# First expert rows by selection products, inverse roots on POOL

## The reference

```python
h = h + concat([pool_out, ssd_out]) @ w_out          # two mixers over rmsnorm(h) @ w_in
h = h + _hier_moe(_rmsnorm(h, norm_ffn), ...)        # top-1 of 4 groups, top-2 of its 8 experts
gate = sigmoid(_rmsnorm(h, norm_ple) @ ple_gate_w + ple_gate_b)
h = h + gate * (p @ ple_proj_w)
y = _rmsnorm(h, norm_final)
# _rmsnorm(x, g) = x * rsqrt(mean(x * x) + 1e-6) * g
```

## Time and profile before

| | |
|---|---|
| median of 3 runs | 585.47 us (584.82 to 586.27) |
| the profiled execution | 585.49 us |
| its span, first to last instruction | 583.6 us |
| mean granted TensorE clock | 0.958 |
| busy: TensorE, DVE, ACT, POOL | 510.3 (87%), 209.7 (36%), 170.7 (29%), 92.6 us (16%) |
| chain that ended last, share of the span | PE 72%, DMA 11%, DVE 8%, SP's queue 3%, ACT 3% |
| DMA moved | 144.72 MB, mean 248 GB/s |

### The profile page before, as it was taken

How to read it: one execution, slowest core, us unless ns; L and a number is a source line. 1 busy time by engine, 2 the same in 40 slices (tenths; PEclk the granted TensorE clock), 3 DMA queues, 4 the chain that set the end, 5 groups by cost and what they waited for, 6 DMA issues and landing times.

```text
span 583.6 us, 7814 instructions
## 1 busy us (share of the span) xinstructions
PE 510.3 (87%) x3098; PEld 314.5 (54%) x3098; DVE 209.7 (36%) x516; ACT 170.7 (29%) x345; POOL 92.6 (16%) x138
## 2 busy tenths in 40 slices
PE   2999978999999997099999999977849999799993
PEld 2888866768654655065555555533425553344452
DVE  2185694423022655441211221111111120565375
ACT  0635233203422423102222222221211223435255
POOL 1000053995000001101111112101111222000000
PEclk9999997999999999579999999999998999799998
DMA  8980000500629804949999999999999997700011
GB/s 322 417 238 2 1 1 0 217 2 19 212 95 419 352 2 182 414 151 356 417 419 416 414 414 418 414 416 418 416 404 388 414 411 293 295 2 0 1 74 72
DMA packets 39638, 144.72 MB, mean 248 GB/s; under 512 B 14458, under 2 KB 15098, under 8 KB 29988
## 3 DMA queue, kind: packets, MB, share of 16 engines
q1 hardware_dynamic: 32740, 132.79, 57.4%
q0 software_dynamic: 5152, 8.85, 4.1%
q10 hardware_dynamic: 1712, 2.62, 1.2%
HBM read 140.15 MB, written 14.19 MB: 264 GB/s over the span
## 4 chain that ended last, share of the span: by engine, by line
PE 72%; DMA 11%; DVE 8%; SPq 3%; ACT 3%; issue 2%; POOL 0%; POOLq 0%; DVEq 0%; ACTq 0%
PE PS L991 17%; PE PS L635 10%; PE PS L823 9%; PE PS L1012 9%; PE PS L1093 7%; PE PS L595 6%; PE PS L606 5%; DMA mem<-in_exp_w_down 5%; DVE mem L1871 2%; SPq L486 2%; PE PS L836 2%; DMA mem<-in_w_a 2%; DMA u_rows<-mem 2%; DVE mem L1615 1%; DMA mem<-u_rows,idx_all 1%
## 5 line engine op out<-in xcount | busy, mean ns | idle before, releaser
L991 PE MATMUL PS<-mem 128*64 128x256 f32 x512 | 118.8, 385 | 7.0 <-DVE mem L1871 7.0
L992 PE MATMUL PS<-mem 128*64 128x256 f32 x512 | 118.8, 385 | 0.0
L991 PEld LDWEIGHTS PS<-mem 128*64 128x64 f32 x512 | 68.2, 138 | 43.1 <-DVE mem L1871 7.9
L1012 PE MATMUL PS<-mem 128*64 128x512 f32 x256 | 62.6, 610 | 18.0 <-issue 8.9
L635 PE MATMUL PS<-mem 128*128 128x260 f32 x320 | 73.9, 387 | 0.0
L992 PEld LDWEIGHTS PS<-mem 128*64 128x64 f32 x512 | 68.2, 138 | 0.0
L635 PEld LDWEIGHTS PS<-mem 128*128 128x128 f32 x320 | 60.3, 192 | 10.7 <-issue 1.5
L595 PEld LDWEIGHTS PS<-mem 128*128 128x128 f32 (+4 forms) x254 | 33.3, 178 | 53.7 <-issue 36.3
L595 PE MATMUL PS<-mem 128*128 128x128 f32 (+4 forms) x254 | 42.6, 303 | 21.1 <-DMA mem<-u_rows,idx_all 12.6
L823 PE MATMUL PS<-mem 128*128 128x512 f32 x128 | 56.6, 595 | 0.0
L1875 DVE TENSOR_TENSOR mem<-PS,mem 64x256 f32<-64x256 f32 x32 | 13.7, 428 | 119.3 <-ACT mem L1291 119.3
(11 more groups left out here) (284 smaller groups left out, 541.4 us busy)
## 6 DMA issues: line engine op xcount, KB each, us to landing
mem<-in_exp_w_down SPq DMA_DIRECT2D x32, 1024.0 KB, 23.0
mem<-in_exp_w_gate SPq DMA_DIRECT2D x32, 1024.0 KB, 16.8
mem<-in_exp_w_up SPq DMA_DIRECT2D x32, 1024.0 KB, 20.2
mem<-in_w_out SPq DMA_DIRECT2D x2, 2048.0 KB, 7.6
mem<-in_ple_gate_w SPq DMA_DIRECT2D x1, 4096.0 KB, 30.3
mem<-choice_rows SPq DMA_DIRECT2D x4, 1024.0 KB, 8.3
mem<-in_xT SPq DMA_DIRECT2D x2, 1040.0 KB, 8.1
mem<-in_w_a SPq DMA_DIRECT2D x2, 1024.0 KB, 11.1
```

What stands on the lines that cost most here:

```text
L991: pe.matmul(PS[0][0:S, 0:FF], rows_k, gu[slot][:, k, :], start=(k == 0), stop=(k == KT - 1))
L992: ins = pe.matmul(PS[1][S:2 * S, 0:FF], rows_k, gu[slot][:, KT + k, :], start=(k == 0), stop=(k == KT - 1))
L1012: ins = pe.matmul(PS[4 + h][h * S:(h + 1) * S, :], actT[:, s % 2, f * S:(f + 1) * S], dn[slot][:, f, h * 512:(h + 1) * 512], start=(f == 0 ...
```

## The change

Three things. The rows of pair 0 no longer come from memory: for each token tile DVE writes a 0/1 matrix times the row's inverse root (`first_pair_rows`, which tells for each of 128 places which token sits there), and TensorE multiplies h1 by it (`first_pair`), which selects, scales and transposes at once, summed over the tiles in banks 0 and 2, which `first_pair_zero` clears. The slot table is summed in bank 3, not in 1. Gather 0 is left out, the second pair is transposed whole within block 1, and what concerns extra blocks moves behind block 0. And all inverse roots are an addition and a power of -0.5 on POOL; ACT's squares carry the 1/1024 in their scale. The order of the tail on ACT and DVE changes with it. The diff, cut (left out are semaphore names, the same wait in the loop by `gathers`, the body of `extra_choices`, which is L1829 to L1850 unchanged, and the tail's squares, which change as `half_square` does):

```diff
+def gathers(p):
+    return 16 * ((p + 1) // 2)
+
...
+C_POWER = C_EPS + 1
...
+        junk_h = at(R_g + D, D)
+        sel = at(R_g, NT, 2 * S)
+        selk = at(R_g + NT * 2 * S, 2, 2, S)
+        hit = at(R_g + (NT + 2) * 2 * S, 2, S)
...
+                        ins = pe.matmul(PS[3][q * S:(q + 1) * S, 0:MAIN], posh[:, j, :], choice[:, q, :],
...
+            SEL = [PS[0], PS[2]]
+
+            def first_pair_zero():
+
+                pe.wait_ge(s_outp_out, 9)
+                for half in range(2):
+                    pe.matmul(SEL[half][:, :], bef[:, 0:1].to_broadcast((P, P)), const[:, 0:256].bitcast(BF16),
+                              start=True, stop=False)
+
+            def first_pair(i, half):
+
+                R = ROWS[ORDER[i]]
+                pe.wait_ge(s_sel_ready, i + 1)
+                for q in range(4):
+                    ins = pe.matmul(SEL[half][:, q * P:(q + 1) * P],
+                                    h1[0:R, ORDER[i], :].rearrange("s (p k) -> s k p", k=KT)[:, 4 * half + q, :], sel[0:R, i, :],
+                                    start=False, stop=(i == NT - 1 and q == 3))
+                if i == NT - 1:
+                    ins.then_inc(s_T_done, 1)
...
             count(3)
             out_half(4, 1, 6, KT)
+            first_pair_zero()
+            first_pair(0, 0)
             h_rows(4, 1)
             route(4)
-            for i in range(NT - 1):
+            first_pair(0, 1)
+            first_pair(1, 0)
+            first_pair(1, 1)
+            count(4)
+            for i in (2, 3, 4):
+                first_pair(i, 0)
+                first_pair(i, 1)
+            for i in range(NT):
                 fill_slots(i)
-            count(4)
-            fill_slots(4)
             count_all()
...
-            pe.wait_ge(g_full[0], 16)
-            pe.wait_ge(s_lg_out, NT)
-            pair_rows(0, 0)
-            pe.wait_ge(s_cnt_taken, 1)
-            pair_rows(0, 1)
-            fill_extra_slots()
             for b in range(HEAD):
                 if b % 2 == 0:
                     pe.wait_ge(s_uT_ready, b + 2)
@@ -1030,9 +1060,17 @@
                     if b >= 2:
                         pe.wait_ge(s_ysb_free, b - 1)
                     down(dn_slot(b - 1), (b - 1) % 2)
-                if b % 2 == 0:
-                    pe.wait_ge(g_full[(b // 2 + 1) % 2], 16 * ((b // 2 + 1) // 2 + 1))
-                pair_rows((b // 2 + 1) % 2, b % 2)
+                if b == 1:
+                    pe.wait_ge(g_full[1], 16)
+                    pe.wait_ge(s_lg_out, NT)
+                    pe.wait_ge(s_cnt_taken, 1)
+                    pair_rows(1, 0)
+                    pair_rows(1, 1)
+                    fill_extra_slots()
+                elif b >= 2:
+                    if b % 2 == 0:
+                        pe.wait_ge(g_full[(b // 2 + 1) % 2], gathers(b // 2 + 1))
+                    pair_rows((b // 2 + 1) % 2, b % 2)
                 pe.wait_ge(s_act_ready, b + 1)
                 act_rows(b)
...
+            root_d = 1.0 / D ** 0.5
 
             act.wait_ge(ld_const, 16)
             for t in range(NT):
                 act.wait_ge(ld_x[t], 16)
-                rms(t, h1[0:ROWS[t], t, :], t, junk, s_rstd_x)
+                A(junk[0:ROWS[t], :], h1[0:ROWS[t], t, :], ACT.Square, scale=root_d,
+                  accum_out=ss[0:ROWS[t], t:t + 1]).then_inc(s_squares, 1)
+                act.wait_ge(s_squares, t + 1)
...
-                step(A(junk[0:R, h * 512:(h + 1) * 512], h1[0:R, t, h * 512:(h + 1) * 512], ACT.Square,
-                       accum_out=ss[0:R, 5 + 2 * i + h:6 + 2 * i + h]))
+                squares = A(junk_h[0:R, h * 512:(h + 1) * 512], h1[0:R, t, h * 512:(h + 1) * 512], ACT.Square, scale=root_d,
+                            accum_out=ss[0:R, 5 + 2 * i + h:6 + 2 * i + h])
                 if h == 0:
-                    step(A(ss0[0:R, i:i + 1], ss[0:R, 5 + 2 * i:6 + 2 * i], ACT.Identity, bias=eps[0:R, :], scale=1.0 / D))
+                    step(squares)
+                    step(A(ss0[0:R, i:i + 1], ss[0:R, 5 + 2 * i:6 + 2 * i], ACT.Identity, bias=eps[0:R, :]))
                 else:
-                    A(rms_[0:R, 5 + t:6 + t], ss[0:R, 6 + 2 * i:7 + 2 * i], ACT.Sqrt, bias=ss0[0:R, i:i + 1], scale=1.0 / D
-                      ).then_inc(s_r_rstd, 1)
+                    squares.then_inc(s_squares, 1)
+                    act.wait_ge(s_squares, NT + i + 1)
 
...
+                    if b == 1:
+                        act.wait_ge(u_stored[0], 48)
+                        act.wait_ge(u_stored[1], 32)
...
-            A(rms_[:, 20:21], eps, ACT.Sqrt)
+            A(ss[:, 20:21], eps, ACT.Sigmoid)
...
+            def inverse_root(R, dst, mean, part, ready):
+
+                step(pool.tensor_tensor(mean, mean, part, ALU.add))
+                pool.tensor_tensor(rstd[0:R, dst:dst + 1], mean, const[0:R, C_POWER:C_POWER + 1], ALU.pow).then_inc(ready, 1)
+
+            for t in range(NT):
+                R = ROWS[t]
+                pool.wait_ge(s_squares, t + 1)
+                inverse_root(R, t, ss[0:R, t:t + 1], eps[0:R, :], s_inverse_root)
...
-            pool.wait_ge(s_r_rstd, NT)
-            step(pool.memset(G, 0.0))
+            for i in range(NT):
+                R = ROWS[ORDER[i]]
+                pool.wait_ge(s_squares, NT + i + 1)
+                inverse_root(R, 5 + ORDER[i], ss[0:R, 6 + 2 * i:7 + 2 * i], ss0[0:R, i:i + 1], s_inverse_root)
+            step(pool.memset(G[:, 1, :], 0.0))
...
-            for p in range(2):
-                gather(p, idx_all[:, p:p + 1])
+            gather(1, idx_all[:, 1:2])
             for p in range(HP + 1):
                 if p >= 2:
                     pool.wait_ge(s_ysb_free, 2 * p - 2)
                     scatter(p % 2, out_all[:, p - 2:p - 1])
                 pool.wait_ge(s_T_done, 2 * p + 2)
-                pool.wait_ge(g_full[p % 2], 16 * (p // 2 + 1))
+                if p == 0:
+                    step(pool.memset(G[:, 0, :], 0.0))
+                else:
+                    pool.wait_ge(g_full[p % 2], gathers(p))
                 gather(p % 2, idx_all[:, p + 2:p + 3])
...
+            for i in range(NT):
+                R = ROWS[TAIL[i]]
+                pool.wait_ge(s_squares, 2 * NT + i + 1)
+                inverse_root(R, 10 + TAIL[i], t_sq[0:R, i, 1:2], t_part[0:R, i:i + 1], s_inverse_root)
+            for i in range(NT):
+                R = ROWS[TAIL[i]]
+                j = 2 if i == NT - 1 else 1
+                pool.wait_ge(s_f_sq3, i + 1)
+                inverse_root(R, 15 + TAIL[i], f_sq[0:R, i, j:j + 1], f_part[0:R, i, j - 1:j], s_inverse_root)
+
...
-                dve.wait_ge(s_rstd_x, t + 1)
-                step(dve.reciprocal(rstd[0:R, t:t + 1], rms_[0:R, t:t + 1]))
+                dve.wait_ge(s_inverse_root, t + 1)
...
-                dve.wait_ge(s_r_rstd, i + 1)
-                last(dve.reciprocal(rstd[0:R, 5 + t:6 + t], rms_[0:R, 5 + t:6 + t]), s_rstd_u, i + 1)
+                dve.wait_ge(s_inverse_root, NT + i + 1)
...
+            def first_pair_rows(i):
+
+                t = ORDER[i]
+                R = ROWS[t]
+                step(tt(hit[0:R], iota_s[0:R, :].unsqueeze(1).to_broadcast((R, 2, S)),
+                        rk[0:R, t, :].unsqueeze(2).to_broadcast((R, 2, S)), ALU.is_equal))
+                for k in range(2):
+                    ins = stt(selk[0:R, k], hit[0:R, k].unsqueeze(1).to_broadcast((R, 2, S)), rstd[0:R, 5 + t:6 + t],
+                              oh[0:R, t, k * NE:k * NE + 2].unsqueeze(2).to_broadcast((R, 2, S)), ALU.mult, ALU.mult)
+                step(ins)
+                tt(sel[0:R, i, :].rearrange("p (q s) -> p q s", s=S), selk[0:R, 0], selk[0:R, 1], ALU.add).then_inc(s_sel_ready, 1)
 
...
             choose(3)
             rank(3)
+            first_pair_rows(3)
             residual(4, 1)
             take_h(4, 1)
             take_logits(4)
             choose(4)
             rank(4)
-
-            dve.wait_ge(s_tab_done, 1)
-            step(ts(out_all[:, 0:MAIN], PS[1][:, 0:MAIN], float(EMPTY), None, ALU.add))
-            ts(idx_all[:, 0:MAIN], out_all[:, 0:MAIN], 1, None, ALU.arith_shift_right).then_inc(s_tab_ready, 1)
-
+            first_pair_rows(4)
             step(tt(ex4, L[:, :, 0:4], gmax[:, :, 0:1].to_broadcast((P, NT, 4)), ALU.subtract))
             tt(e21, ev[:, :, 1], ev[:, :, 0], ALU.subtract).then_inc(s_rt_a, 1)
+
+            def take_rows_of(bank, slot, half):
+                tt(uT[:, slot, half * 512:half * 512 + 512].rearrange("p (k c) -> p k c", c=P), tiles(bank[:, :]),
+                   g_ffn[:, 4 * half:4 * half + 4].unsqueeze(2).to_broadcast((P, 4, P)), ALU.mult).then_inc(s_uT_ready, 1)
+
+            for half in range(2):
+                dve.wait_ge(s_T_done, half + 1)
+                take_rows_of(PS[2 * half], 0, half)
+
+            dve.wait_ge(s_tab_done, 1)
+            step(ts(out_all[:, 0:MAIN], PS[3][:, 0:MAIN], float(EMPTY), None, ALU.add))
```

(50 more changed lines are left out.)

122 lines of the change are left out of this document (40 added, 82 removed).

## The result

The changed kernel takes 582.2 us (median of 14 runs) against 585.5 before: ratio 0.9938, interval 0.9921 to 0.9955. The direction is as predicted, the size is not: 572.1 was forecast, with 569.8 to 578.5 as its range, so 3.3 us came of the 13.4 forecast. The profiled execution has a span of 579.7 us, against 583.6 before.

The account below looks back on a forecast made before the run. The experts were taken as bound by the weight stream up to 437.88 us, by TensorE after. 585.5 - 0.1 (start) - 10.8 (stream) - 2.5 (tail) = 572.1 us, range 569.8 to 578.5.

Parts of the forecast that it names:

- the price of a selection product: First pair on TensorE: eight products per token tile, two records each, 1.9 us a tile, 9.4 us in all.
- down(24): Down product of block 24, where the weight stream stops setting the time: 10.8 us earlier, near 427 instead of 437.88.
- load of block 7 issued: Weight queue: block 7's load, waiting for block 0's slot, issued at 244.4 instead of 257.08, leaving no gap.
- Start: Kernel front, up to the fifth diagonal: five roots in series stay hidden until one costs over 1.4 us; 0.1 us gained.
- rival (a): TensorE's clock falls around 231 as before, slowing tiles 2 to 4, slots and block 0: 578.3 us; chance 0.15.
- rival (b): Gather of the second pair lands three to four us late, putting off block 2: 575.5 us; chance 0.10.
- rival (c): Weight stream doesn't take up lost time, for instance loads stop behind extra_choices; 581.6 us; chance 0.08.
- a hole around 250: Sign in the DMA profile around 250 us that would show rival (c).
- rival (d): POOL's power is expensive in front, routing and tail: equals the gain at 3.0 us, 590 at 3.5; chance 0.04.
- the p of the text: Cost of one root on POOL, add and power with hand-overs: 0.5 us, range 0.4 to 3.
- The text's own formula: Loss from dearer roots in front, routing and tail: 5(p - 1.4) + (p - 1.8) + (p - 0.5) + (p - 1).
- Tail: Last gate product to final scale, Sqrt table loads gone: 3.4 us instead of 6.2, 2.5 us saved after crowding.

Follow-up runs that it names:

- contig: The changed kernel with selection products loading contiguous slices of the token rows as weights (wrong columns, a measurement only): 572.2 us, ratio 0.9777.
- pow4: sel_stat with three more powers in each of the twenty roots, results unused: 590.0 us, ratio 1.0081.
- twice: The changed kernel with every selection product of tiles 2, 3 and 4 done twice (sums doubled): 592.7 us, ratio 1.0137.
- roots_only: The changed kernel with the first pair gathered from memory again, keeping the POOL roots and new tail order: 583.0 us, again 583.7.
- sel_stat: The changed kernel with the selection matrix as weight and token rows streaming past, then copied and transposed: 573.2 us, again 572.4.
- kmajor: sel_stat with token rows and first pair written in the column order the transposes read, making their weight loads contiguous: 572.3 us.

## Why the prediction was wrong, step by step

**The failed step** is the price of a selection product: "a 128-column record is about as long as its load, so I take 1.9 us a tile, 9.4 in all". The load was taken from the earlier trace rows, where the router reads neighbouring columns; the selection reads every eighth. That term of 9.4 measured 20: 80 records at 0.25 us. What went wrong with it is that a load's time was taken by its shape, whatever lies between its columns. With the contiguous load the same 80 take 9.6 (0.89, 2.9 and 5.8), and the rest of the sum then comes true: 572.2 against 572.1. The last tenth is luck, since down(24) comes 0.6 us earlier than worked out and the tail is 0.4 longer. The steps of the prediction beside the changed kernel and contig:

| step | predicted | changed | contig |
|---|---|---|---|
| last selection product ends, us | 239.2 | 247.7 | 238.5 |
| first gate-up | 240.9 | 249.2 | 240.0 |
| load of block 7 issued | 244.4 | 252.9 | 243.7 |
| down(0) ends | 251.5 | 260.2 | 251.0 |
| DMA from 248 to 266, GB/s | near 400 | 239 | 406 |
| down(24) | 427 | 436.5 | 426.4 |
| last gate product to final scale | 3.4 | 3.8 | 3.8 |
| time | 572.1 | 582.2 | 572.2 |

**Start:** five roots in series stay hidden, as said: a root takes 0.8 us and ACT's squares come 1.2 apart. The 0.1 us gained there can't be seen under the spread of the start (225.2 to 227.1). Roots 2.7 apart (pow4) are not hidden.

**Clock, rival (a):** TensorE had products without a break, and its granted clock fell to 0.5 all the same, from 239.4 to 246.2 in the changed kernel. It cost next to nothing there: the loads took 336 ns at either level, and a record 0.243 us (5.82 for 24) before, 0.249 (11.97 for 48) across the fall. In contig it did not fall. What made it fall isn't shown, nor what brought it back: in twice it is at 1.00 from 251 on, while the same stepped loads go on to 259. Block 0 ran at full clock in contig and in the changed kernel, which is where 1.2 of the 2.6 us lead over roots_only at block 7's load come from (3.7 us against 4.9 from the first gate-up to the issue).

**Gather 1, rival (b):** not late. In contig the pair's transposes follow down(0) at once, at 250.93 behind 249.07.

**The stream, rival (c):** the result lies where this rival put it (581.6), but not by its mechanism. Loads did not stop behind extra_choices: down(0) waited 0.49 us for take_act, the 0.4 of the sum. They stopped because nothing had been released by then: its sign, a hole around 250, did show (5 GB/s from 249 to 252), behind a first gate-up that came only at 249.2.

**The power, rival (d):** 0.55 us plus 0.19 for the add, and 0.85 with the hand-overs that the p of the text counts in; it took 0.5. With 1.8 us more in each root the sign did turn (pow4): they cost 17 us, more than the 12 to 13 that sel_stat gains. The text's own formula gives 11 at that p. In proportion 1.3 us more would have been enough, by my estimate a p of about 2.2; the 3.0 of the text was set too high, since the waits in front cost more than their slack suggests.

**Tail:** 2.5 predicted; 2.4 in the trace, 2.5 by roots_only's median. The size is right in part by luck: the sum was 2.8 less 0.3 for the crowded order, and what took the 0.4 was the dearer root at its end (0.85 for 0.5).

**The warning was in the trace of before:** the loads of its transposes, first of token rows (neighbouring columns, 200 to 230), then of gathered rows (every eighth column, 262 to 430); the columns are count, minimum, median and maximum in ns.

```profile
L595 PEld LDWEIGHTS PS<-mem x24: 133/140/222, 200.3 to 227.4; 128*128 128x128 f32 x16, 8*128 8x128 f32 x8
...
L595 PEld LDWEIGHTS PS<-mem x96: 185/193/208, 263.6 to 426.0; 128*128 128x128 f32 x96
```

One line, one shape, 140 against 193 ns: the same line of code at two access patterns. It would have given the sign and not the size, since a transpose pays 53 ns for the step and a selection product 144. I had priced the load by its shape alone. The Trainium skill (TensorE: Matmul & The Clock Gate, "LDWEIGHTS (loading the stationary operand)") does that too: P / 1.2 ns, by the column count P and not by the rows. For 128 columns I estimate 107 ns from that. The rows hardly matter here either (8 rows 329 ns, 128 rows 336), and the bf16 loads of the count take 106, but the time is 190 for contiguous f32 and 336 for stepped, so the measurement decides.

## What to carry to other kernels

Price a product by the access pattern of its weights as well as by its shape: a 128x128 f32 load with columns 4 or 8 elements apart took 330 ns instead of 190, and with 128 moving columns that made a record 0.25 us instead of 0.12. In a transpose the same step cost less, 193 instead of 140. Where weights would be stepped, look for an order in which the other operand is the weight, as in sel_stat: per tile two products of 512 columns replaced eight with stepped weights and gave 9 to 10 us. There both operands of the selection are contiguous and the step is left to eight transposes; what a stepped moving operand costs no run shows. When an earlier start is to fill a hole in a weight stream, follow it past the first load, as long as loads find the queue empty.

## What was not expected of the hardware

- From 4 to 8 elements the step between columns does not matter: both cost about 330 ns at a granted clock of 1.00, 1 costs 192. (2 elements: 331, seen only at 0.50.)
- A stepped load of a selection product takes the same 336 ns at a granted clock of 1.0 and of 0.5. Others do not: before, contiguous ones of 64 columns took 0.14 and 0.23 us.
- With TensorE busy in every microsecond, but held by such loads, the granted clock fell from 1.0 to 0.5 for some 7 us (239.4 to 246.2 in the changed kernel). In twice it came back while they went on, so the loads alone don't explain it.
- ACT and DVE pay for a step too (kmajor against sel_stat, writes 128 elements apart): ACT's copy of a row of 1024 columns took 2.07 us instead of 1.15, the copies of 512 columns from PSUM 1.33 instead of 0.69 on DVE and 1.34 instead of 0.60 on ACT.
